# One layer with gathered experts: order of the sync engine's queue and of six row fetches in the routing stage

## The reference

```python
idx = jnp.take_along_axis(cand_i, pos, axis=-1)          # 512 x 8 x 16
gate = jax.nn.softmax(best_s, axis=-1)
...
act = gelu(einsum('tkd,td->tk', u_tab[ib], xb))           # rows of u, one per pick
out = einsum('tk,tkd->td', act * gb, v_tab[ib])           # rows of v
```

## Time and profile before

| what | us |
|---|---|
| median of 3 runs | 1517.12 (1516.35 to 1518.38) |
| the profiled execution, its own time | 1515.29 |
| its span, first to last instruction | 1513.6 |
| TensorE busy | 1450.1 (96%) |
| VectorE busy | 1245.1 (82%) |
| ScalarE busy | 830.8 (55%) |
| GpSimd busy | 505.5 (33%) |
| moved by DMA | 420.50 MB, 278 GB/s on the mean |

### The profile page before, as it was taken

The page is one execution under the profiler, slowest core; times in us unless marked ns, Lnnn a source line. Parts: engine busy times, 40 slices in busy tenths (PEclk is TensorE's granted clock), DMA queues, the critical chain, the costliest instruction groups (busy, mean ns, idle before and its releaser), DMA issues.

```text
span 1513.6 us, 25263 instructions
## 1 busy us (share of the span) xinstructions
PE 1450.1 (96%) x9438; PEld 1310.6 (87%) x9438; DVE 1245.1 (82%) x2383; ACT 830.8 (55%) x1571; POOL 505.5 (33%) x425
## 2 busy tenths in 40 slices
PE   6999789999998999999989989999999999999999
PEld 6898678779998999999989889999888878888787
DVE  4538778674799699899669939999999989999997
ACT  4453454133244578778768744444566555655663
POOL 4111630010176877777621103232222222222210
PEclk9999899999999999999999999999999999999999
DMA  5230001421156799999899999998999999999993
GB/s 189 91 100 1 8 30 46 152 97 71 57 201 237 262 332 343 373 344 339 291 380 358 399 354 352 380 378 328 392 410 409 412 410 410 411 409 410 406 407 133
DMA packets 168872, 420.50 MB, mean 278 GB/s; under 512 B 12945, under 2 KB 100145, under 8 KB 152241
## 3 DMA queue, kind: packets, MB, share of 16 engines
q1 hardware_dynamic: 126064, 234.06, 42.5%
q0 software_dynamic: 27712, 167.82, 28.3%
q10 hardware_dynamic: 14976, 17.05, 3.2%
HBM read 372.44 MB, written 46.40 MB: 277 GB/s over the span
## 4 chain that ended last, share of the span: by engine, by line
PE 39%; DMA 15%; DVE 12%; issue 4%; ACT 2%; POOL 2%; SPq 0%; ACTq 0%; DVEq 0%; POOLq 0%
DMA v_raw<-in_peer_v 10%; PE bank L2101 6%; PE bank L2096 6%; PE bank L2097 6%; PE bank L2118 3%; PE bank L2427 3%; PE bank L2429 3%; PE bank L2428 3%; DVE v_lo L2503 2%; DMA u_raw_more<-in_peer_u 2%; PE bank L2415 2%; PE bank L2416 2%; PE bank L2417 2%; DVE pair_sum L1822 2%; DVE v_lo_late L2503 1%
## 5 line engine op out<-in xcount | busy, mean ns | idle before, releaser
L2096 PE MATMUL bank<-x_hi,u_split 128*128 128x320 f32 x832 | 255.1, 319 | 2.9 <-ACT u_split L2156 2.9
L2097 PE MATMUL bank<-x_lo,u_split 128*128 128x320 f32 x832 | 248.5, 311 | 0.0
L1798 POOL DMA_INDIRECT scores<-in_peer_uv,pair_index x86 | 105.8, 1230 | 379.5 <-DVE pair_sum L1822 375.4
L2474 ACT ACTIVATE act_tile<-onehots 128x384 f32<-128x384 f32 x128 | 124.5, 972 | 76.2 <-DVE act_lo L2516 72.9
L2096 PEld LDWEIGHTS bank<-x_hi,u_split 128*128 128x128 f32 x832 | 159.3, 191 | 3.9 <-issue 3.9
L2097 PEld LDWEIGHTS bank<-x_lo,u_split 128*128 128x128 f32 x832 | 158.6, 191 | 0.0
L2101 PE MATMUL bank<-x_hi,u_split 128*128 128x320 f32 x832 | 140.7, 311 | 5.0 <-POOL u_split L2003 5.0
L2101 PEld LDWEIGHTS bank<-x_hi,u_split 128*128 128x128 f32 x832 | 128.0, 190 | 5.6 <-POOL u_split L2003 5.6
L2003 POOL TENSOR_TENSOR u_split<-u_raw,u_split 128x1024 fp32r<-128x1024 f32 x41 | 99.4, 2426 | 93.8 <-DVE u_split L2003 58.2
L2427 PE MATMUL bank<-v_hi,act_hi 128*128 128x512 f32 x304 | 120.0, 395 | 2.9 <-DVE v_lo L2503 2.7
L2429 PE MATMUL bank<-v_hi,act_lo 128*128 128x512 f32 x304 | 119.2, 392 | 0.0
(11 more groups left out here) (434 smaller groups left out, 4022.8 us busy)
## 6 DMA issues: line engine op xcount, KB each, us to landing
v_raw<-in_peer_v SPq DMA_DIRECT2D x128, 512.0 KB
u_raw<-in_peer_u SPq DMA_DIRECT2D x64, 512.0 KB
u_raw_more<-in_peer_u SPq DMA_DIRECT2D x64, 512.0 KB, 5.9
gates<-gate_stage SPq DMA_DIRECT2D x24, 1024.0 KB
onehots<-gates SPq DMA_DIRECT2D x32, 768.0 KB
early_gelus<-early_gelu ACTq DMA_DIRECT2D x104, 160.0 KB
gelu_tile<-early_gelus SPq DMA_DIRECT2D x104, 160.0 KB
w_raw<-in_w_in SPq DMA_DIRECT2D x9, 1024.0 KB, 5.0
```

The lines of the kernel that those rows point to most:

```text
L1798: pool.indirect_dma_start(self.slot(k), None, self.table, bass.IndirectOffsetOnAxis(ap=self.sidx[:, k:k + 1], axis=0)).then_inc(self.lande ...
L2096: nc.tensor.matmul(out, uh[:, q, w], m.xh[:, k, P + NS:], start=(k == 0), stop=False)
L2097: nc.tensor.matmul(out, uh[:, q, w], m.xl[:, k, P + NS:], start=False, stop=False)
L2474: nc.scalar.activation(af[n % 2][:], gt[:, it % 2, :, jj], ACT.Copy).then_inc(gate_cols, 1)
```

## The change

Two edits in `routing`. In SP's queue, the loads of the first two batches are issued ahead of the loop, and batch n's place in the loop has the loads of batch n+2, so that a store stands behind the loads of the two batches that follow it. On POOL, the six first row fetches stand one behind each of the low parts 13 to 18, where they stood together behind low part 13.

```diff
                 for n in range(2, FIRST + NU):
                     load_u(n)
+                AHEAD_U = 2
+                for n in range(AHEAD_U):
+                    for t in ups_of[n]:
+                        load_u(t + NU)
                 for n in range(NB_):
-                    for t in ups_of[n]:
+                    for t in ups_of[n + AHEAD_U] if n + AHEAD_U < NB_ else []:
                         load_u(t + NU)
                     if n % 2:
                         store_gates(n)
...
                     if t == TURN_1 + 3:
                         up_rows.wait_moved(pool)
-                        for k in range(fetched):
-                            up_rows.fetch(pool, k)
+                    if TURN_1 + 3 <= t < TURN_1 + 3 + fetched:
+                        up_rows.fetch(pool, t - TURN_1 - 3)
```

## The result

The kernel with both edits takes 1507.09 us (median of 4 runs, 1506.05 to 1510.45), the kernel before, in 4 runs beside it, 1517.75. The ratio is 0.9933, with a 95% interval of 0.9919 to 0.9946: faster, by 10.7 us. The prediction was 1506.0, its range 1499 to 1512. The profiled execution took 1506.98 us with a span of 1505.2, 8.4 us less than the span of before.

What follows compares the result with a forecast made beforehand. TensorE was taken to set the pace from 408 to 760 us, full DMA engines from 760 to 885 and in the experts; gains 7.2 + 4 = 11.2 us gave 1505.9, called 1506 us, range 1499 to 1512.

Steps and rivals of the forecast that it cites:

- Part one: Spreading six row fetches on POOL removes TensorE's hole near 461 us: 7.2 us gained, bounds 4.35 and 7.2.
- The upper bound: At TensorE's hole, both the 4.35 us wait and the 2.8 us of lower-clock ups go: 7.2 us gained.
- The slot's overrun: On POOL, a fetch with 0.3 us issue overruns its idle slot by 0.14 us, 0.8 us over six.
- The store rival: Before 760 us, evictions wait for later gates stores, seven times; 1525.5 us at a 12 us landing; chance 0.07.
- It just fits: Store 7, issued near 590.3, lands within 4.3 to 9.3 us, before the eviction at 599.52; costed at nothing.
- the margin of 9.2 us: Time left for store 7 to land, from its issue near 590.3 to the eviction of batch 10 at 599.52.
- The rival's price: For landing time L, evictions before 760 us wait L - 9.2, seven times; 19.6 us at L = 12.
- Part two: Loads ahead of stores in SP's queue shorten late routing, 760 to 885 us: 4 us gained, bounds 0 and 13.3.
- the rate: Over late routing, 760 to 885 us, 47.9 MB pass at 398 GB/s instead of 383: 4.7 us, rounded to 4.
- then the bytes: Sign of a wrong forecast: late-batch evictions waiting for gates stores mean bytes, not order, decide; no size given.
- only part one shows: Full DMA engines from 760 us replace load waits with equally long gather or store waits: 1509.9 us; chance 0.27.
- All late loads vanish: Late routing nears the experts' rate and load waits go: 8.5 to 13.3 us, 1496.6 to 1501.4 us; chance 0.13.

Runs made afterwards that it cites:

- half stores: Both edits, late gates stores writing 64 of 128 partitions and eight early stand-in stores filling the rest, against the kernel before: 1503.46 us, ratio 0.9898.
- the fetches alone: Only the six row fetches spread, SP's queue put back, against the kernel before: 1511.11 us, ratio 0.9951; again, 1510.87 us, ratio 0.9942.
- the loads alone: Only the loads ahead of the stores, the six fetches put back together, against the kernel before: 1515.21 us, ratio 0.9978.

## Why the prediction was right, and which step of it was off

**Part one was right in size and cause.** 7.17 us were predicted; up to low part 83, 7.20 were measured, and within 0.04 us of that in eight further runs with the fetches spread (the ninth, half stores, opened the hole again). The upper bound held: the clock dip went with the wait. The slot's overrun was smaller than the 0.8 us allowed for, since the issue takes 0.17 us: 0.03 us for each of the six. The later landing cost nothing: the sixth fetch goes out at 473.67 (473 was predicted), and VectorE's wait for the seventh row even fell, from 12.3 to 5.4 us.

**The store rival.** "It just fits" was wrong, and the margin of 9.2 us did not hold. Store 7 went out at 583.34, and the eviction that waited for it ran 11.4 us later:

```profile
583.34 0.43 SPq L2033 DMA_DIRECT2D gates<-gate_stage  x1
```
```profile
594.76 0.60 ACT L2192 ACTIVATE gate_stage<-bank 128x512 f32<-128x512 f32 x1 [2.67 <-DMA gates<-gate_stage]
```

So a landing was longer than the 9.3 us that the prediction read as its upper bound. The store waits that the rival names came: 7 of the 12 lie before 752 us, 13.7 us in all, 2.7 the longest. They cost nothing: TensorE's waits from 405 to 760 us come to 1.0 us, and none is for ScalarE. The rival's price, the excess once in each cycle, left out its own objection, ScalarE's idle time; 2.7 us over the limit seven times would have been up to 19 us by it. Putting this term at nothing was right for one of the two reasons given, the idle time, and not for the other.

**Part two is the term that was mis-sized: 4 us predicted, 1.3 measured** in the profiled executions of before and after. Both edits against the fetches alone on one chip give 1.3 by the medians and 2.5 by the profiles; the loads alone give 3.4 with an interval from 1.5 to 5.2. The 1.3 of the first pair is hardly above the noise of such a sum; that part two is more than nothing is shown by the interval of the loads alone. So some 1 to 3.4 us is what can be said, and the times by themselves do not exclude the 4. The step that failed is the rate: 398 GB/s was taken over the 125 us from the 50 us in which the kernel before ran at it. The prediction's own window found 390, and 386 over the same work, 7.2 us earlier; by its own arithmetic 47.9 MB take 122.8 us at 390 GB/s, a gain of 2.2, and 124.1 us at 386, a gain of 0.9. Three things stand in the way of 398. The wait for a load at the head went, and waits for two stores of 10.50 us in sum came. The middle, 53.5 us, holds 52.5 us of VectorE's work, which no order of the loads takes out of it. The load behind the last store still waits at the tail, as was forecast, but for 7.91 us and not 3.52. Store waits in the late batches were named as the sign of "then the bytes", and that is what they were.

**The rivals.** The mechanism of "only part one shows" came nearer to the late stretch than the forecast's: waits for loads were replaced by waits for stores of the same length. Its time, 1509.9, is 2.8 us above the median measured, that of the forecast 1.1 below. That the sum came out so close is in part luck: with the two sizes of the traces, 7.2 and 1.3, it would have given 1517.1 - 8.5 = 1508.6, and no trace shows the other 1.5 us. The rule of the Trainium skill weighed there, in "DMA: Bandwidth & Descriptors", section "Issuing engines are not separate DMA queues", says that the transfers of all engines run on the same 16 DMA engines; no edit here moved a transfer to another engine, so no run here shows it. "All late loads vanish" is excluded: ScalarE still waits 7.91 us for a load, and the late stretch got 1.3 us shorter, not 8.5 to 13.3.

**What stays open.** The two profiled executions differ by 8.3 us in their own times, the medians by 10.7; the kernel before lies 2.5 us below its median in its profiled one. Where the runs without a trace spend the rest can't be read. How much of the tail the bytes alone set was tried only by halving stores, which also makes each store land sooner; the two were not parted. The profile of the loads alone is of an execution of 1519.77 us, 4.6 above that kernel's median, so its stages may not stand for the median.

## What to carry to other kernels

A stall on an engine that is full on both sides of it was worth its wait and the slower work behind it (4.35 us of waiting cost 7.17, 1.86 cost 3.67), and both can be read from the spacing of one event per step. Reordering a queue in a stretch where the DMA engines were full moved a wait, for the most part, from the late transfer to whatever then stood behind it: ask first whether bytes leave the stretch, and how long the longest run of busy work of another engine in it is, for no order shortens that. Cost a new wait against the idle time of the engine that bears it, and not once in each cycle.

## What the runs showed of the hardware

A store of 1 MB in 2048 pieces took 18.9 us from issue to landing when six gathers of 1 MB were issued beside it; among the ups one took 11.4 us, from 583.34 to 594.76. SP's own issue of the load behind such a store was held 8.73 us, as it was 6.85 and 8.86 before, so what stands ahead in SP's queue also delayed the issue of the next transfer. On POOL an issue took 0.17 us of idle time behind a low part, not the 0.30 of a fetch behind a fetch.
